# Experts: the turn of the inner rows placed between the halves of the side up product, in the second layer between the halves of the summing product

## The reference, cut to what matters

```
def expert_block(args):
    xblk, e = args
    u = jax.nn.silu(xblk @ w1[e]) * (xblk @ w3[e])
    return u @ w2[e]
```

## Time and profile before

| | us |
|---|---|
| median of 3 runs | 1540.88 (1540.47 to 1541.53) |
| the profiled execution | 1544.08 |
| its span in the profile | 1542.1 |
| first layer's experts | about 663 to 932 |
| second layer's experts | about 1315 to 1536 |

### The profile page before, as it was taken

One profiled execution on the slowest core, in us unless ns is written; L12 is line 12 of the kernel. 1 busy time (PEld: TensorE's weight loads), 2 busy tenths in 40 slices (PEclk: granted clock), 3 DMA queues, 4 the chain that ended last, 5 costly groups with the idle time before them and its releaser, 6 DMA issues. The chain is left out here.

```text
span 1542.1 us, 17006 instructions
## 1 busy us (share of the span) xinstructions
PE 1445.8 (94%) x6200; PEld 718.8 (47%) x6200; DVE 757.9 (49%) x1689; ACT 277.6 (18%) x570; POOL 165.9 (11%) x156
## 2 busy tenths in 40 slices
PE   6999999789999999999999999899989999999987
PEld 2544644344444444632323233765777875433332
DVE  4297866646555879532122223686676635211112
ACT  3201101422232210411011011110242203000000
POOL 0000011001011210021111101001001210111000
PEclk9999999989999999999999999999999999999999
DMA  9420234101223453689999986425333695999996
GB/s 380 186 98 27 74 145 164 55 28 55 82 82 141 164 191 109 275 322 420 423 425 422 418 360 237 162 85 225 127 110 137 220 374 211 379 418 412 422 420 238
DMA packets 49536, 355.55 MB, mean 231 GB/s; under 512 B 6288, under 2 KB 6672, under 8 KB 22704
## 3 DMA queue, kind: packets, MB, share of 16 engines
q1 hardware_dynamic: 41360, 330.79, 54.3%
q0 software_dynamic: 4800, 14.24, 2.5%
q10 hardware_dynamic: 3296, 9.44, 1.6%
HBM read 343.88 MB, written 10.56 MB: 230 GB/s over the span
## 5 line engine op out<-in xcount | busy, mean ns | idle before, releaser
L1209 PE MATMUL ps<-hT,ring 128*128 128x512 f32 (+1 forms) x1344 | 452.6, 492 | 1.9 <-DVE hT L2334 1.3
L1209 PEld LDWEIGHTS ps<-hT,ring 128*128 128x128 f32 x1344 | 253.8, 192 | 177.0 <-issue 157.9
L1515 PE MATMUL ps<-ring,m 128*64 128x512 f32 x624 | 277.1, 595 | 12.7 <-ACT m L1958 8.0
L1515 PEld LDWEIGHTS ps<-ring,m 128*64 128x64 f32 x624 | 81.9, 137 | 185.4 <-issue 172.7
L2296 DVE SCALAR_TENSOR_TENSOR spare<-ring,crow 128x1024 bf16<-128x1024 f32 x120 | 155.8, 1298 | 4.1
L1222 PE MATMUL ps<-ring,hT 128*128 128x512 f32 (+1 forms) x352 | 125.1, 515 | 0.0
L2021 POOL TENSOR_TENSOR wide<-wide,gates 128x512 f32<-128x512 f32 (+1 forms) x48 | 69.6, 1450 | 395.9 <-DVE gates L2473 395.9
L1517 PE MATMUL ps<-n_,m 128*64 128x512 f32 x224 | 100.0, 595 | 0.0
L1310 PE MATMUL ps<-yT,ring 128*128 128x512 f32 (+1 forms) x256 | 94.5, 492 | 2.3 <-ACT n_ L1857 2.3
L1517 PE MATMUL ps<-wide,m 128*64 128x512 f32 x208 | 93.7, 597 | 0.0
L1222 PEld LDWEIGHTS ps<-ring,hT 128*128 128x128 f32 x352 | 66.7, 190 | 55.1 <-issue 51.4
(11 more groups left out here) (389 smaller groups left out, 1699.3 us busy)
## 6 DMA issues: line engine op xcount, KB each, us to landing
ring<-w SPq DMA_DIRECT2D x39, 2048.0 KB, 11.1
ring<-win SPq DMA_DIRECT2D x52, 1024.0 KB, 4.9
ring<-wmod SPq DMA_DIRECT2D x48, 1024.0 KB, 5.0
n_<-w SPq DMA_DIRECT2D x13, 2048.0 KB
hT<-w SPq DMA_DIRECT2D x13, 2048.0 KB, 16.6
wide<-w SPq DMA_DIRECT2D x13, 2048.0 KB
ring<-wbr SPq DMA_DIRECT2D x8, 1024.0 KB, 4.8
ring<-wout SPq DMA_DIRECT2D x4, 2048.0 KB, 11.9
```

The costliest lines, as they stand in the source:

```text
L1209: last = pe.matmul(b[:, 0:W], w[:, k, jj * P:(jj + 1) * P], hT[:, k, 0:W], start=(k == 0), stop=(k == KD - 1))
L1515: pe.matmul(ps[0:HALF, bnk, :], left[:, k, 0:HALF], even[k], start=(k == 0), stop=(k == n_k - 1), skip_group_check=True)
```

## The change

In the first layer the side up product is cut between its second and third k step, and `turn_u(e)` stands between. In the second layer `mix(e - 1)` moves from between gate and up to behind up, and `turn_u(e)` stands between its first two products (tokens 0 to 127) and its last two. Pair 0 of the second layer has no summing product and keeps its order, and so does the last summing product.

```diff
-                    def four_quarters(bnk, left, quarters):
+                    def four_quarters(bnk, left, quarters, ks=range(4)):
 
-                        for k in range(4):
+                        for k in ks:
...
-                    def mix_block(first, last_, signal=True):
-                        for t in range(live(l)):
+                    def mix_block(first, last_, signal=True, tiles=range(live(l))):
+                        for t in tiles:
...
-                    def mix(e):
+                    def mix(e, turn=None):
...
-                        mix_block(e == 0, e == PAIRS - 1).then_inc(y_mixed, 1)
+                        mix_block(e == 0, e == PAIRS - 1, True, range(0, 1))
+                        if turn is not None:
+                            turn_u(turn)
+                        mix_block(e == 0, e == PAIRS - 1, True, range(1, 2)).then_inc(y_mixed, 1)
...
                             four_quarters(7, side_xT, split_k(wg, wg2)).then_inc(side_gate_done, 1)
-                        if not side and e:
-                            mix(e - 1)
                         weights_landed("w3", e)
...
-                            four_quarters(6, side_xT, split_k(wu, wu2)).then_inc(side_up_done, 1)
+                            four_quarters(6, side_xT, split_k(wu, wu2), range(0, 2))
+                            turn_u(e)
+                            four_quarters(6, side_xT, split_k(wu, wu2), range(2, 4)).then_inc(side_up_done, 1)
...
                         gate_and_up(e)
-                        turn_u(e)
+                        if not side and e:
+                            mix(e - 1, e)
+                        elif not side:
+                            turn_u(e)
```

## The result

| | before | after |
|---|---|---|
| median, compared on the same chips | 1544.31 us (9 runs) | 1550.54 us (9 runs) |
| ratio of after to before | | 1.0046 (95% interval 1.0028 to 1.0064) |
| profiled execution | 1544.08 | 1550.07 |
| its span | 1542.1 | 1548.1 |

The kernel got slower by 0.46%, some 7 us. The forecast was 6.5 us slower, with the median at 1547.4 and the range up to 1549.8. The measured median lies 0.7 us above that range, because the kernel before itself measured 1544.3 over these nine runs and not the 1540.9 of the three runs on which I had put the sum. Applied to 1540.88, the ratio gives 1548.0. All ratios in this text leave out two slow runs, one of e3 at 2083.75 us and one of e4 at 2202.28 us.

The account below looks back on a forecast made before the run. The matrix engine's own order was taken to bound the first layer, the stream of weights the second. +5.6 and +0.9 made +6.5 us, added to the median of 1540.88: 1547.4 us, range 1543.0 to 1549.8 for 8 in 10.

Parts of the forecast that it names:

- The level: Whole kernel: the median of 1540.88 us, to which the forecast difference of +6.5 us was added.
- both terms: First layer's experts +5.6 us (3.5 to 7.2) and second layer's +0.9 us (-1.5 to +1.3).
- the 1.95 us: First layer: interval from the side up's last group to down, claimed to stay at 1.95 us.
- The turn in the stream: First layer: the moved transposes take 0.7 us of the matrix engine's time per pair, eight pairs, +5.6 us.
- the price: First layer: estimated cost of the moved turn per pair, 0.7 us, bounds 0.44 to 0.9, with two tiling changes.
- Case (d): First layer: edit costs nothing, transposes slip between groups; only the second layer's 0.9 remains, 1541.8 us; chance 0.05.
- Gate to up: Second layer, last pair: gate start 1504.86 to up, which waits for w3 until 1514.3; 9.44 us forecast.
- Up to down: Second layer, last pair: up, then half the summing product, turn, other half, before down; 6.48 + 4.96 = 11.44 us.
- (b): Second layer gains at most 3.1 us, as a fixed stream end allows; with first layer's 5.6, 1543.4 us; chance 0.12.
- (c): Second layer's weight stream follows the releases, giving the full 10.5 us; 1536.0 us in all; chance 0.07.
- (e): First layer: inserted transposes cost over 0.9 us a pair; over 1549.5 us in all; chance 0.04.

Follow-up runs that it names:

- e3: Kernel before with the first layer's part of the change, plus ScalarE copying the turned rows ahead of the side up's lower half; ratio 0.9972.
- e4: Kernel before with only ScalarE's order changed, turned rows copied ahead of the side up's, turn left in place; ratio 1.0009.
- e1: Kernel before with only the first layer's part of the change, second layer as before; ratio 1.0048.
- e5: Kernel before with only the second layer's part of the change, and lighter weight loads there from pair 1 on; second layer's stage 181.53 us, one run.
- e6: Kernel before with only the second layer's weight loads made lighter from pair 1 on; second layer's stage 195.79 us, one run.
- e7: Kernel before with the second layer's part of the change in pairs 1 to 6 only, pair 7 as before; 1540.07 us, one run.
- e8: Kernel before with the second layer's summing product in three parts: between gate and up, before the turn, behind the turn; ratio 0.9999.
- e9: Kernel before with e3's first layer and e8's second layer together; ratio 0.9958.
- e10: Kernel after, with the change in both layers, plus ScalarE copying the turned rows ahead of the side up's; ratio 0.9972.
- e11: The same kernel as e9 run again, unchanged, compared against the kernel before; ratio 0.9970.

## Why the prediction was right or wrong

**The level was wrong.** The step that failed is the one that adds the difference to the median of 1540.88. Three runs that agree within 1.1 us looked like a fixed level. Over 9 to 35 runs on each of four occasions the same kernel had medians of 1544.3 to 1545.5, from 1539.0 to 1550.8. These 88 runs fall into two groups: 29 lie at 1539.0 to 1542.5 and 59 at 1543.3 or more, with 0.9 to 2.8 us between the groups in each set, and my three were all of the lower one. Why there are two isn't shown. Nothing in the range stood for that: its upper end is 1540.88 with both terms at their upper ends (+8.5) and 0.4 more. With 3 us more it would have held the time. The profiled execution, 3.2 us above the median shown, was a sign of it that I noted and then left out.

**The first layer: right, by its own steps.** The turn waits for nothing, the 1.95 us stay, L1958 stands 0.03 us behind the side copy, all as written. The turn in the stream: 0.70 forecast, 0.72 measured, eight times, 5.8 us for 5.6. The drain at a change of tiling mode, which the Trainium skill states (TensorEngine Tiling (Array Packing), Key Properties), fits the rows: 0.54 us from the last group to the transposes, where 0.43 is the usual step, and 0.58 to the next group. By count the edit adds one such change per pair and not two, since the one from the turn to down gives way to one from the side up to down; but that place lies inside a wait, and two changes are in the stream, as the price had it. Case (d) falls by e1; the reason itself is shown by e3 and e4.

**The second layer: right in sum, off in two terms that cancel.** Gate to up 9.79 us, 9.44 forecast: the last w3 came 0.35 later than I had worked out from the neighbours' landings. Up to down 11.09, 11.44 forecast. Of this 0.16 is the turn: the rows show it and the summing product both as 128*128, and the turn costs 0.43 there (1528.54 to 1528.97), not the 0.59 carried over from the side block's turn. The other 0.20 is a slip in my sum: half of a summing product of 3.64 us is 1.82, as measured twice, and not 1.92. For these reasons, and since the longer steps into and out of the old place went too (0.52 and 0.48 us where 0.43 is the usual one), a pair won 2.0 us and not 1.5. That the sum of the two, 20.88, was measured as forecast (9.44 + 11.44) is luck.

**Rivals.** (b) and (c) needed a last gate that moves forward, and it didn't: from the stage's first copy to the last tanh it is 181.1 us before and 181.3 after, and e5 with e6 shows that the stream is what holds it: (c)'s gain exists, 14 us, once the weights are lighter. The ceiling of 435 GB/s by the Trainium skill (DMA: Bandwidth & Descriptors, Bandwidth) would have left room for 4%; the trace kept to 416. (e) falls by 0.72.

**What is left open.** Start to first tanh and the stretch between the two layers differ by 1.3 and -2.1 us between the two profiles. Both are untouched by the change, and the second goes with the granted clock (below). The first varies most: in the profiled executions of e6 and e7 the first tanh came at 666.8 and 666.5 us, in the eleven others at 670.5 to 672.5, with the same program up to there. That is about the distance between the two groups of runs; that it is their cause is not shown.

## What to carry to other kernels

When an engine waits for a copy, look at what stands ahead of that copy in its own engine's order, before moving the producer: here the producer moved, the copy didn't, and 0.7 us a pair that had been hidden became visible. Two chains that end within 0.1 us of each other have to be shortened together. And in a stage whose transfers run without a gap, look at the last block first: here time won in the blocks before it was only waited away (e7). A better order of the last block didn't show in the whole either (e8), for another reason, the clock. Last, three runs that agree are not yet a level.

## What the runs showed of the hardware that was not expected

The stretch from the last side up copy of the first layer to the first copy of turned rows in the second holds the same work in all kernels. In the profiled executions it took 405.2 to 411.5 us. Its mean granted clock goes with it: 1.00 in e3 (405.5 us), 0.99 in before (410.3), 0.98 in e9 (411.5). The difference is as much as the whole effect of the change, and it is why a stage's own time told more here than the whole.

Where the matrix engine had stood still for weights for some us, the granted clock often fell shortly after it set off again. After the 3.12 us wait that ended at 1479.96 in the kernel after:

```profile
1475.00:1480.00 5.00, 1.88 (x12) 0.45 (x9) 0.00 (x0) 0.60 (x1) 0.00 (x0) 1.00 1.02 411
1480.00:1485.00 5.00, 5.00 (x16) 1.89 (x18) 0.00 (x0) 0.00 (x0) 0.00 (x0) 0.66 1.03 396
```

It fell too behind the 3.54 us wait of the kernel after and the 3.6 us one of e3. In e5 and e6, which wait for no weights in the second layer, and in the kernel before, whose longest wait is 2.56 us, it stayed at 1.00 from 1330 us to the last result. But the length of the wait alone isn't the rule: e10 kept 1.00 behind waits of 3.04 and 3.14 us, and ahead of the last gate the wait was 2.56 in before, with 1.00 behind it, and 2.6 in e8 and e11, with 0.66 to 0.73. In e1, whose second layer is that of the kernel before, the clock was 0.66 from 1366 to 1371 us, behind a wait of 1.23 us for VectorE; the same wait in before left it at 1.00, and that pair took 1.7 us longer in e1 (28.51 for 26.80). An order that makes the matrix engine faster than its weights can so lose a little more than the wait itself. What decides it was not tried.
